# Opening of a two-layer decoder step by column halves of its input, root products moved, end copies counted by engine

## The reference

```python
def rmsnorm(x, g):
    xf = x.astype(jnp.float32)
    y = xf * lax.rsqrt(jnp.mean(xf * xf, axis=-1, keepdims=True) + RMS_EPS)
    return (y * g.astype(jnp.float32)).astype(x.dtype)
# layer 0:  proj = rmsnorm(x, norm_mix_g[0]) @ w_in[0]   (1024 x 2048)
# last:     y_prompt = rmsnorm(xp, norm_out_g); y_sample = rmsnorm(xs, norm_out_g)
```

## Time and profile before

| | us |
|---|---|
| median of three runs | 1908.63 |
| lowest, highest | 1903.7, 1911.07 |
| the profiled execution, its own time | 1901.55 |
| its span in the profile | 1900.0 |
| mean granted clock of TensorE in it | 0.981 of full speed |

### The profile page before, as it was taken

How to read it: one execution, slowest core, us unless ns; L and a number is a source line. 1 busy time by engine, 2 the same in 40 slices (tenths; PEclk the granted TensorE clock), 3 DMA queues, 4 the chain that set the end, 5 groups by cost and what they waited for, 6 DMA issues and landing times.

```text
span 1900.0 us, 38089 instructions
## 1 busy us (share of the span) xinstructions
PE 1806.1 (95%) x15237; PEld 1665.9 (88%) x15237; DVE 938.4 (49%) x1415; ACT 593.2 (31%) x1102; POOL 233.4 (12%) x350
## 2 busy tenths in 40 slices
PE   5997898899999999999979999999999999999998
PEld 4995665689999999999868888878889999999998
DVE  5335676445444343534434454576774534344444
ACT  3114555433222121231333353363223222222222
POOL 3512333211000000020000000003002000000002
PEclk9998999899999999999989999999999999999999
DMA  6228999514776766625147747743132676522221
GB/s 194 75 84 281 328 332 318 191 45 155 265 243 232 253 242 242 243 89 200 58 137 239 240 156 239 238 151 112 46 108 77 211 251 241 213 90 88 89 79 59
DMA packets 176173, 338.83 MB, mean 178 GB/s; under 512 B 10698, under 2 KB 117892, under 8 KB 174445
## 3 DMA queue, kind: packets, MB, share of 16 engines
q1 hardware_dynamic: 163573, 216.18, 34.6%
q0 software_dynamic: 12480, 120.97, 17.6%
HBM read 324.33 MB, written 100.19 MB: 223 GB/s over the span
## 4 chain that ended last, share of the span: by engine, by line
PE 85%; DVE 6%; DMA 4%; ACT 2%; issue 2%; SPq 1%; POOLq 0%; POOL 0%; DVEq 0%; ACTq 0%
PE pp L636 53%; PE pp L882 16%; PE pp L696 2%; PE pp L992 2%; DMA vring<-in_cache_b_kv 2%; PE pp L1039 2%; PE pp L1005 1%; PE pp L733 1%; PE pp L709 1%; DVE rnorm L1169 1%; PE pp L1020 1%; DMA out_new_d_prompt<-pt_l 1%; ACT e_p L1913 1%; PE pp L682 1%; PE pp L1064 1%
## 5 line engine op out<-in xcount | busy, mean ns | idle before, releaser
L1741 ACT ACTIVATE whi<-raw 128x1024 fp32r<-128x1024 f32 x208 | 220.6, 1061 | 868.3 <-PE pp L636 723.7
L636 PE MATMUL pp<-a_hi,whi 128*128 128x288 f32 x1280 | 277.3, 298 | 10.3 <-DVE wlo L1141 5.6
L636 PE MATMUL pp<-a_lo,whi 128*128 128x288 f32 x1280 | 276.4, 298 | 0.0
L1141 DVE TENSOR_TENSOR wlo<-raw,whi 128x1024 fp32r<-128x1024 f32 x208 | 258.4, 1242 | 36.0 <-ACT whi L1741 36.0
L636 PE MATMUL pp<-a_hi,wlo 128*128 128x288 f32 x1280 | 276.2, 298 | 0.0
L636 PE MATMUL pp<-b_hi,whi 128*128 128x288 f32 x1280 | 274.4, 296 | 0.3 <-DVE zbuf L1414 0.3
L636 PE MATMUL pp<-b_lo,whi 128*128 128x288 f32 x1280 | 274.1, 296 | 0.0
L636 PE MATMUL pp<-b_hi,wlo 128*128 128x288 f32 x1280 | 274.1, 296 | 0.0
L636 PEld LDWEIGHTS pp<-a_hi,whi 128*128 128x128 f32 x1280 | 208.3, 190 | 11.4 <-DVE wlo L1141 6.3
L636 PEld LDWEIGHTS pp<-a_hi,wlo 128*128 128x128 f32 x1280 | 208.6, 191 | 0.0
L636 PEld LDWEIGHTS pp<-a_lo,whi 128*128 128x128 f32 x1280 | 208.4, 191 | 0.0
(11 more groups left out here) (242 smaller groups left out, 2118.6 us busy)
## 6 DMA issues: line engine op xcount, KB each, us to landing
out_new_d_sample<-in_cache_d_kv POOLq DMA_DIRECT2D x32, 2040.0 KB, 8.5
kring<-in_cache_b_kv SPq DMA_DIRECT2D x128, 256.0 KB, 4.6
vring<-in_cache_b_kv POOLq DMA_DIRECT2D x128, 256.0 KB, 4.9
raw<-in_w_up SPq DMA_DIRECT2D x32, 1024.0 KB, 5.4
raw<-in_w_down SPq DMA_DIRECT2D x32, 1024.0 KB, 5.2
kring<-in_cache_d_kv SPq DMA_DIRECT2D x104, 256.0 KB, 3.1
vring<-in_cache_d_kv SPq DMA_DIRECT2D x104, 256.0 KB, 4.4
raw<-in_w_in_cd SPq DMA_DIRECT2D x24, 1024.0 KB, 5.3
```

Of the source, the lines that this page charges most:

```text
L636: last = pe.matmul(acc_h[s][:, h, :], w[s][:, k, :], m[:, k, NH * h:NH * h + NH], start=(at_ == 0 and n == 0), stop=(at_ == KT_N - 1 and n ...
L1141: dve.tensor_tensor(wlo_v[j], raw_v[q // 2][:, :, j, :], whi_v[j].bitcast(F32), ALU.subtract).then_inc(wlo_ready, 1)
L1741: act.activation(whi_v[j], raw_v[q // 2][:, :, j, :], ACT.Copy).then_inc(whi_ready, 1)
```

## The change

In words:

- **Loads.** The gain loads move to ACT's queue. SP first loads only the 128 columns `ident` of the constants, then the column half 0 of x (prompt and sample), waits for `ident`, issues weight unit 0, waits for half 0, issues half 1, then unit 1, and behind it the rest of the constants and the other small loads.
- **Transposes.** Tiles 0 to 3 need only half 0. Three PSUM buffers (`pp[1]` to `pp[3]`) replace two. The transposes of tiles 4 to 7 stand inside output tile 0, before its products of k = 0 to 3. The gains are transposed between tiles 1 and 2.
- **Root.** ACT squares x with tokens in rows (ten instructions of up to 128 x 512 with a running sum) in place of eight squares of 128 x 576, and POOL adds nothing. DVE works on 5 columns (scale, add, reciprocal), writes a diagonal matrix of 128 x 512 and one of 64 x 64, and PE multiplies ones by it (`token_root`), which spreads the reciprocal roots over the partitions in `pp[2]`. This stands inside output tile 1, before its k = 5. DVE copies the row out (`row_root`) before it takes tile 0.
- **Moved behind the first four output tiles:** lambda on DVE, its exponential on ACT. ACT loads the table of the square root in the opening with a one-column dummy. POOL's first loads of cache values no longer stand behind its additions.
- **Ending.** POOL sums seven tiles; the row sums of these and of the eighth tile's squares are two sets of six products, the first between the transposes of y tiles 6 and 7 of block 0. `yt_done` becomes `yt_act` and `yt_dve`; a block waits only for its transposes, and PE for the block that used its PSUM buffer.

The diff, cut to its core:

```diff
@@ sp
-            for m, n in enumerate(("norm_mix_g", "norm_mlp_g")):
-                sp.dma_start(gain_rows[16 * m:16 * m + 16, :],
...
-            sp.dma_start(con[:, :], a["consts"]).then_inc(s_const, 16)
-            sp.dma_start(x_tok[:, 0:4, :], a["x_prompt"][0].rearrange("(t p) d -> p t d", p=P)).then_inc(s_x, 16)
-            sp.dma_start(x_tok[0:NS, 4, :], a["x_sample"].rearrange("b t d -> (b t) d")).then_inc(s_x, 16)
+            sp.dma_start(con[:, 0:P], a["consts"][:, 0:P]).then_inc(s_const, 16)
+            half_x(0)
+            sp.wait_ge(s_const, 16)
             unit(w_ab, 0, 0, 0, wait=False)
+            sp.wait_ge(s_x2[0], 32)
+            half_x(1)
             unit(w_ab, 256, 1, 1, wait=False)
+            sp.dma_start(con[:, P:NC_], a["consts"][:, P:NC_]).then_inc(s_rest, 16)
@@ pe
+            def transpose_x(k):
+                if k % 4 == 0:
+                    pe.wait_ge(s_x2[k // 4], 32)
+                if k >= 3:
+                    pe.wait_ge(x_ready, k - 2)
...
+            def token_root():
+                pe.wait_ge(s_rest, 16)
+                pe.wait_ge(r0_diag, 1)
+                pe.wait_ge(x_ready, 8)
+                pe.matmul(pp[2][:, 0:SEQ], ones, diag0[:, 0:SEQ], start=True, stop=True)
+                pe.matmul(pp[2][:, SEQ:N], ones[0:NS, :], diag0[0:NS, SEQ:N], start=True, stop=True).then_inc(ms_ready, 1)
+            def opening(n):
+                if n < 4:
+                    transpose_x(n + 4)
+                if n == KT_N + 5:
+                    token_root()
+            transpose_x(0)
+            transpose_x(1)
+            pe.wait_ge(s_gain, 96)
+            pe.transpose(bank[0][:, 0:57], gain_rows[0:57, :], ident[0:57, 0:57]).then_inc(gain_ps, 1)
+            transpose_x(2)
+            transpose_x(3)
-            dense(lambda i: i, 1, ahk, alk, a_ready, 0, hook=mean_square(0), peel=True)
+            dense(lambda i: i, 1, ahk, alk, a_ready, 0, peel=True, before=opening)
@@ pe, ending
+            transpose_result(0, range(KT_N - 1))
+            pe.wait_ge(sqs_done, 8 * 3 + 7)
+            row_sums(sqsum, bank[4])
+            transpose_result(0, range(KT_N - 1, KT_N))
+            pe.wait_ge(xsq_ready, 8 * 4)
+            row_sums(zbuf[:, N:2 * N], bank[5])
@@ dve
+                if k == 1:
+                    dve.wait_ge(gain_ps, 1)
+                    dve.tensor_copy(gains[:, 0:57], bank[0][:, 0:57]).then_inc(gain_ready, 1)
...
-                if k in (5, 7):
-                    split_lo(0, k // 2 - 2)
+                if k in (2, 5):
+                    split_lo(0, k // 3)
+            def row_root():
+                dve.wait_ge(ms_ready, 1)
+                link(dve.tensor_copy(rnorm[:, :], pp[2][:, 0:N]))
+            token_root()
+            dense(lambda i: i, 1, to_proj(), peel=True, hook=row_root)
@@ dve, ending
                 dve.wait_ge(yt_ps, t + 1)
-                dve.wait_ge(yt_done, t)
@@ act
+            act.activation(dummy_a[:, :], ident[:, 0:1], ACT.Sqrt)
+            square_x(0)
             act.wait_ge(gain_ready, 1)
+            for k in range(KT_N):
+                fin_post(0, G_MIX, x_ready, 0, square=False)(0, 0, k)
+                if k in (1, 4):
+                    split_hi(0, k // 4)
+                if k < 4:
+                    square_x(k + 1)
+                elif k > 4:
+                    square_x(k)
+            square_x(8)
+            square_x(9)
@@ pool
-            sum_squares(0)
...
-            sum_squares(4)
+            sum_squares(4, KT_N - 1)
```

More of the change, by code:

```diff
@@ L188, in build @@
         sqsum = at("sqsum", W_TMP + 5 * N, N)
-        dummy = at("dummy", total - 8, 1)
+        dummies = at("dummies", total - 8, 8)
+        dummy, dummy_a = dummies[:, 0:1], dummies[:, 1:2]
         con = at("con", W_CONST, NC_)
@@ L622, in _, with dense @@
         def _(pe):
-            def dense(group, n_groups, m_hi, m_lo, ready, ready_base, hook=None, peel=False, order=range(KT_N)):
+            def dense(group, n_groups, m_hi, m_lo, ready, ready_base, hook=None, peel=False, order=range(KT_N),
+                      before=None):
                 def four(G, first):
@@ L631, in four @@
                         for at_, k in enumerate(order):
+                            if before and first:
+                                before(KT_N * q + at_)
                             if first and q == 0:
@@ L1112, in transpose_result, with row_sums @@
                                         y_feat[:, N * k + P * t:N * k + P * t + rows], ident)
[L1113 to L1122, removed]
+                if ks[-1] == KT_N - 1:
+                    last.then_inc(yt_ps, 1)
+            def row_sums(src, bk):
+                for t in range(5):
+                    rows = P if t < 4 else NS
+                    pe.matmul(bk[0:rows, t:t + 1], src[:, P * t:P * t + rows], ones[:, 0:1], start=True, stop=True)
+                pe.matmul(bk[NS:P, 4:5], src[:, SEQ:N], ones[:, 0:1], start=True, stop=True).then_inc(ms_ready, 1)
+            transpose_result(0, range(KT_N - 1))
[4 more added lines that the diff above has]
+            row_sums(zbuf[:, N:2 * N], bank[5])
             pe.wait_ge(acc_free, 2 + T_END)
@@ L1839, in sample_attention @@
                         other_work(NB0 * b + i)
-            act.wait_ge(gain_ready, 1)
[L1843 to L1849, removed]
+            for m, n in enumerate(("norm_mix_g", "norm_mlp_g")):
+                act.dma_start(gain_rows[16 * m:16 * m + 16, :],
+                              a[n].rearrange("l (k p) -> (l k) p", p=P)).then_inc(s_gain, 16)
@@ new lines, in _, with square_x @@
+            act.dma_start(gain_rows[32:40, :], a["norm_out_g"].rearrange("(k p) -> k p", p=P)).then_inc(s_gain, 16)
+            act.dma_start(gain_rows[40:44, :], a["a_scale"][0].rearrange("(k p) -> k p", p=P)).then_inc(s_gain, 16)
+            act.dma_start(gain_rows[44:56, :], a["c_conv_w"][0].rearrange("j (k p) -> (j k) p", p=P)).then_inc(s_gain, 16)
+            act.dma_start(gain_rows[56:57, :], a["b_subln_g"]).then_inc(s_gain, 16)
+            def square_x(n):
+                h, t = n // 5, n % 5
+                rows = P if t < 4 else NS
+                if t == 0:
+                    act.wait_ge(s_x2[h], 32)
+                    act.wait_ge(q_zero, 1)
+                if n:
+                    act.wait_ge(r0_sums, n)
+                act.activation(square0[0:rows, :], x_tok[0:rows, t, 512 * h:512 * h + 512], ACT.Square,
+                               accum_out=sums0[0:rows, h, t:t + 1]).then_inc(r0_sums, 1)
@@ L1850, in _ @@
+            square_x(9)
+            act.wait_ge(v_ready, 1)
+            act.activation(r_tok0, r_tok0, ACT.Sqrt).then_inc(sqrt_ready, 1)
+            dense(lambda i: i, 1, peel=True)
             act.wait_ge(lam_d, 1)
             act.activation(lam_t[:, 130:132], lam_t[:, 128:130], ACT.Exp).then_inc(lam_e, 1)
-            dense(lambda i: i, 4, peel=True, hook=root(0))
+            dense(lambda i: i + 1, 3)
             token_major(0)
@@ L2029, in _ @@
                 act.wait_ge(yt_ps, t + 1)
-                if t:
-                    act.wait_ge(yt_done, t)
                 act.activation(y_tok[0:rows, t, :], y_ps[t][0:rows, :], ACT.Copy,
-                               scale=r_tok[0:rows, t:t + 1]).then_inc(yt_done, 1)
+                               scale=r_tok[0:rows, t:t + 1]).then_inc(yt_act, 1)
         @block.gpsimd
```

89 lines of the change are left out of this document (50 added, 39 removed).

## The result

| | before | after |
|---|---|---|
| median | 1906.18 (6 runs) | 1890.21 (6 runs) |
| lowest, highest | 1903.7, 1911.07 | 1877.61, 1894.1 |
| ratio of the means, 95% interval | | 0.9908 [0.9879, 0.9936] |
| profiled execution, its span | 1901.55, 1900.0 | 1877.61, 1876.0 |
| mean granted clock | 0.981 | 0.983 |

What follows compares the result with a forecast made beforehand. PE, 95% busy, was taken as the bound, so only the opening and the ending could gain: 13.3 + 0.9 = 14.2 us, off the median 1908.63, gives 1894.4 us. The range was 1890.5 to 1901.5.

Steps and rivals of the forecast that it cites:

- Opening, 13.3 forecast: From the kernel's start to PE's start of tile 2: 49.53 before, 36.2 forecast, a gain of 13.3 us.
- half 0 at 7.4: Opening: the first column half of x is loaded at 7.4 us against 15.2 before, bounds 6.8 and 9.5.
- the return of the clock at 22.4: Opening: PE's clock rises from 1.2 to 2.4 GHz at 22.4 us, expected between 19.5 and 25.
- the diagonal at 30.5: Opening, root: DVE's diagonal matrix is ready at 30.5 us, hidden by 1.4 before PE reaches it at 31.95.
- tile 2 at 36.2: End of the opening: PE starts output tile 2 at 36.2 us instead of 49.53.
- The first rival: Opening: clock stays low while transposes are mixed in; tile 2 at 40.55, gain 9.0 + 0.9, time 1898.7; chance 28%.
- half 0 was not interleaved: Rival on the opening's loads: half 0 and unit 0 share the engines, half 0 at 9.5, 2.1 us lost; chance 5%.
- the shift did not stop at sample attention: Rival: the earlier start is lost at the memory-held sample attention, only 0.9 and some left, time 1906; chance 5%.
- the attention did not stay at the low clock: Rival: the clock stays low in sample attention, so the kernel is slower, 1918 at 48 us of low clock; chance 4%.
- Ending, 0.9 forecast: From the last product to the end: the stream of stores starts 0.9 us earlier, bounds 0.3 and 1.8.
- A set of row sums: Ending: each set priced at 1.25 us, the second ending at 1888.7, not 1889.6, which gives the 0.9.
- The counts: Ending: per-engine counts let blocks overlap, but were given no gain because the stores are a continuous stream.

Runs made afterwards that it cites:

- e1: The changed kernel with the old ending put back, so only the opening is new; 1893.59 us, ratio 0.9944 to the kernel before.
- e8: The changed kernel with the single count `yt_done` put back in the ending, the two sets of row sums kept; 1889.8 us (one run).
- e7: The changed kernel with all eight tiles of x transposed ahead of the first product, not within output tile 0; 1894.08 us (one run).
- f2: The changed kernel, unchanged, profiled and timed once more beside the kernel before; 1890.08 us, ratio 0.9929 to the kernel before.
- e5: The changed kernel plus idle identity products, 12 before the first transpose and 8 in PE's wait for the first `wlo`; 1885.93 us (one run).
- f3: The changed kernel plus idle identity products (12, then 8) and tile 4's transposes ahead of the first product; 1889.12 us, ratio 0.9929 to the kernel before.
- e6: The changed kernel with the transposes of tile 4 moved ahead of PE's wait for the first `wlo`; 1885.11 us (one run).

## Why the prediction was right and where not

**Opening, 13.3 forecast; 12.9 (13.8 in e1, 13.6 in e8).** The steps: half 0 at 7.4 was 8.1, within its bounds; 0.4 of the lost 0.7 was regained by the small steps up to the first `wlo` (forecast 15.9, measured 16.17). The first product at 17.3 came at 17.6; the return of the clock at 22.4 came at 21.9; tile 0's end at 27.85 came at 28.4; the diagonal at 30.5 came at 29.9 and was hidden by 2.7, not 1.4; the root's products, taken at 1.49 from start to last result, took 1.38; tile 2 at 36.2 came at 36.65. That the clock's return lies so near the forecast is luck in part: in the three other profiles with this opening it came at 19.6, 20.0 and 21.3. The 49.53 itself is one profile: the second one of before has 49.03, and with the second one of after the gain is 12.6.

**The first rival, that the clock stays low amid transposes, did not happen.** The pace rose with transposes mixed in, in every profile with this opening, between 19.6 and 21.9. The Trainium skill (TensorE: Matmul & The Clock Gate, part 4) says that transposes do not count as PE being busy for the full clock. The trace of e7 agrees for transposes alone, 5.4 us of them in a row at the low level, and the window at 1894 of the earlier trace rows does not; the one at 163 says less than I took from it, since eight products of 128 x 512 ran on PE from 156.4 to 158.3. A mixture, which has products as well, does not refute the page. The rival that I had built at 28% on the eleven us at 433 ns is refuted. My own ground against it, that the transposes of before had pauses between them, is weakened by e7, which has none. The other three rivals: half 0 was not interleaved (8.1, not 9.5); the shift did not stop at sample attention (340.2 against 340.7); the attention did not stay at the low clock.

**Ending, 0.9 forecast, 1.7 measured.** Two terms were mis-sized, both on the same side. A set of row sums was taken at 1.25, the price of one that starts after a wait of PE; here, behind other work of PE, the two take 1.00 and 1.02 (1863.76 to 1864.76, 1865.02 to 1866.04), so the row sums gave 1.24. The counts, taken at nothing because the stores are one stream, gave 0.45: the stream is the bound in after, but with the relay it was not yet full.

**Sum.** Forecast 14.2; by the stages 14.6 with the two first profiles and 14.3 with the two second ones; by timed runs 16.0 between medians and 17.5 by the ratio in the first series, 10.3 and 13.5 in the second. The mechanism of the opening and the size of the whole were right; the ending was half of what it gave, inside its bounds of 0.3 and 1.8.

**The time.** This is where the prediction failed: 1890.21 lies 0.3 below the range and 4.2 below the forecast of 1894.4, by two steps. First, "I put the same difference on their median": 1908.63 was the middle of three runs, and six give 1906.18. Of the 4.2, 2.45 are this base and 0.8 the ending; the opening takes 0.4 back, and some 1.4 are scatter between runs. With 1906.18 as base the same forecast and range would have been 1892.0 and 1888.1 to 1899.1, and the result inside. Second, the range was built of the bounds of the edits alone, as if the kernel's own time were exact: its lower end was "both upper bounds with some luck". The same code ran from 1874.7 to 1893.0 on one chip in f2, and the kernel before from 1893.6 to 1911.9 beside it. Two stages that the change does not touch differ by as much between profiles: an MLP that is ten us shorter in some executions, and the stage of sample attention that varies by twelve. Three runs within 7 us gave no sign of it, but the profiled execution at 1901.55, below all three, did, and I noted it and drew nothing from it.

## What to carry to other kernels

An earlier input is worth what the next chain behind it lets through: here the loads alone gave 7.3 of some 13 until the sums of squares left GpSimd. The order in which PE does work that it has to do anyway may move the return of its clock: with twenty transposes ahead of all products (e7, one profile) a head start of 1.5 us was lost. Idle products ahead of a wait did not keep the clock (e5), and idle products that PE must finish first stood in the way of its real ones (f3, first product 3.1 later than in e6). Before a range is given for a change of one per cent, the kernel's own spread goes into it, and a difference between two profiles is cut into stages that both share, so that what the change did is not mixed with what the chip did that time.

## What the hardware showed unexpectedly

Long unbroken runs of identical products at a granted clock of 1.00 ran at one of two mean distances, 133.3 ns (three of about 131, one of 140) or 130.0 ns (128 and 132 in turn), each setting in behind a pause of PE: 397 to 399 us or 387 to 389 for 2976 products, 3 of 26 MLP stretches at the shorter. The granted-clock column reads 1.00 in the windows of after between 16 and 22 while transposes and products last as long as at 1.2 GHz (1.41 for five transposes, against 0.64 from 22.14 on), and in e5, where PE had been warmed before, it reads 0.50 in the same place with the same durations: there a pace has to be read from durations, not from the column.
